# A two-block layer on one Trainium2 core: first unit in pieces of 1 to 4 rows behind zero products, later norm, earlier rotation tables, k as the third unit

## The reference

```python
u = rmsnorm(h, g_mix[i])
proj = u @ w_in[i]
q, k, v, z, xbc, dt_raw, g_a, g_s = jnp.split(proj, offsets, axis=-1)
q = apply_rope(q..., positions)
k = apply_rope(k..., positions)
attn = sliding_window_sink_attention(q, k, v, sinks[i])
```

## Time and profile before

| | us |
|---|---|
| median of 3 runs | 2734.81 |
| lowest, highest | 2734.21, 2738.23 |
| the profiled execution's own time | 2736.75 |
| its span | 2734.9 |
| PE busy | 2702.9 |
| DVE busy | 1961.5 |
| ACT busy | 1412.4 |

### The profile page before, as it was taken

One profiled execution on the slowest core, in us unless ns is written; L12 is line 12 of the kernel. 1 busy time (PEld: TensorE's weight loads), 2 busy tenths in 40 slices (PEclk: granted clock), 3 DMA queues, 4 the chain that ended last, 5 costly groups with the idle time before them and its releaser, 6 DMA issues.

```text
span 2734.9 us, 41656 instructions
## 1 busy us (share of the span) xinstructions
PE 2702.9 (99%) x16606; PEld 2375.4 (87%) x16606; DVE 1961.5 (72%) x2946; ACT 1412.4 (52%) x2092; POOL 105.5 (4%) x197
## 2 busy tenths in 40 slices
PE   8999999999999999999999999999999999999998
PEld 7888888888888888888888899998888888888887
DVE  7668777757777776677766778877787775677764
ACT  6455556544555554455544552257665553455543
POOL 1320000000000000000000000000000000000000
PEclk9999999999999999999999999999999999999999
DMA  7566556555578888877856556973455556555554
GB/s 241 168 206 208 179 177 207 187 189 188 185 238 281 286 279 299 293 279 277 278 201 213 176 184 223 314 264 116 139 185 190 192 194 191 186 188 185 187 194 143
DMA packets 168914, 581.58 MB, mean 213 GB/s; under 512 B 20128, under 2 KB 26992, under 8 KB 168208
## 3 DMA queue, kind: packets, MB, share of 16 engines
q1 hardware_dynamic: 152368, 526.06, 57.4%
q0 software_dynamic: 16208, 52.85, 5.2%
q10 hardware_dynamic: 144, 0.01, 0.0%
HBM read 535.06 MB, written 43.09 MB: 211 GB/s over the span
## 4 chain that ended last, share of the span: by engine, by line
PE 93%; DVE 3%; DMA 2%; ACT 1%; issue 1%; POOL 0%; SPq 0%; DVEq 0%; ACTq 0%; POOLq 0%
PE PS L957 92%; DVE wl L1922 1%; DMA raw<-in_w_in 1%; PE PS L1295 0%; DVE SQA L1922 0%; DVE H L1922 0%; DVE QT L1922 0%; ACT wh L1380 0%; DMA RO<-KT 0%; PE PS L1122 0%; DMA raw<-in_w_down 0%; ACT AHt L1380 0%; DMA KDU<-KT 0%; DVE CC L1930 0%; DMA H<-in_xT 0%
## 5 line engine op out<-in xcount | busy, mean ns | idle before, releaser
L1922 DVE TENSOR_TENSOR wl<-raw,wh 128x1024 fp32r<-128x1024 f32 (+3 forms) x888 | 1039.8, 1195 | 447.9 <-ACT wh L1380 446.1
L1380 ACT ACTIVATE wh<-raw 128x1024 fp32r<-128x1024 f32 (+3 forms) x888 | 894.3, 1031 | 521.7 <-PE PS L957 407.9
L957 PE MATMUL PS<-CHt,wh 128*128 128x512 f32 x2816 | 885.8, 395 | 0.0
L957 PE MATMUL PS<-BIGt,wh 128*128 128x512 f32 (+1 forms) x2816 | 756.0, 356 | 1.8 <-issue 0.6
L957 PE MATMUL PS<-AHt,wh 128*128 128x512 f32 (+1 forms) x2080 | 636.0, 386 | 11.4 <-DVE wl L1922 11.3
L957 PEld LDWEIGHTS PS<-CHt,wl 128*128 128x128 f32 x2816 | 529.0, 188 | 124.8
L957 PE MATMUL PS<-CHt,wl 128*128 128x256 f32 x2816 | 553.5, 278 | 0.0
L957 PEld LDWEIGHTS PS<-BIGt,wl 128*128 128x128 f32 x2304 | 435.4, 189 | 79.0 <-issue 0.2
L957 PE MATMUL PS<-BIGt,wl 128*128 128x256 f32 x2304 | 498.4, 279 | 0.0
L957 PEld LDWEIGHTS PS<-BIGt,wh 128*128 128x128 f32 x2816 | 434.9, 190 | 6.5 <-issue 3.8
L957 PEld LDWEIGHTS PS<-AHt,wl 128*128 128x128 f32 x1952 | 367.8, 188 | 79.8 <-issue 0.7
(11 more groups left out here) (311 smaller groups left out, 1632.0 us busy)
## 6 DMA issues: line engine op xcount, KB each, us to landing
raw<-in_w_up SPq DMA_DIRECT2D x264, 512.0 KB, 5.0
raw<-in_w_in SPq DMA_DIRECT2D x196, 512.0 KB, 4.1
raw<-in_w_down SPq DMA_DIRECT2D x132, 512.0 KB, 4.3
raw<-in_w_gate SPq DMA_DIRECT2D x88, 512.0 KB, 5.5
raw<-in_w_down SPq DMA_DIRECT2D x56, 384.0 KB, 3.5
PKR<-in_w_in SPq DMA_DIRECT2D x36, 512.0 KB, 5.2
parked_halves<-PKH POOLq DMA_DIRECT2D x36, 512.0 KB, 5.7
parked_halves<-PKL POOLq DMA_DIRECT2D x36, 512.0 KB, 7.0
```

What stands on the lines that cost most here:

```text
L957: return e.matmul(o, l, r, start=start, stop=stop, skip_group_check=True)
L1380: return e.activation(o, x, f, **k)
L1922: return e.tensor_tensor(o, x, y, op)
```

## The change

The first unit is cut into seven pieces of 1, 1, 2, 4, 4, 2 and 2 rows (`FIRST`) in place of four of 4, and the loads of x are cut the same way; the first two of x are issued by ScalarE, the others by SyncE between the weight loads. PE begins with three products of a tile of zeros (`WARM`), which GpSimd fills first. GpSimd's loads of constants wait for the last of x, where they waited for its second quarter. The norm and the first unit's finish stand five pieces after its end (`QHOLD`), the second unit's finish two. The rotation tables are put in the same lane as the sums of x, behind them. k is the third unit; the bank pairs keep their order, so that k gets (2,0). The turned copies of q and k get slots to match (`TURN_Q`), and some semaphores are merged.

```diff
+FIRST = (1, 1, 2, 4, 4, 2, 2)
+WARM = 3
-QHOLD = 3
+QHOLD = 5
...
-    for i in range(4):
-
-        add("w_in", 0, 16, 256 * i, "U1", "ev_q", i, mode=order(i), mid=(("norm", 0, 0),) if i == 0 else (), hold=QHOLD if i == 0 else 0,
-            banks=((0, 1), (3, 4), (2, 0), (1, 3))[i],
-            gens=([2, stage("rotary", 0, 3)] if i == 0 else []) + [("rope_q", i, [None] * (0 if i else 2) + [0, None, 1])])
-    add("w_in", 0, 16, 1024, "U1", "ev_k", 0, mode="turn", banks=(4, 2), gens2=[stage("full_u1", 0, 4)], gens=[("rope_k", 0, [0, None, 1, 2, None])])
+    first_banks = iter(((0, 1), (3, 4), (2, 0), (1, 3), (4, 2)))
+    for what in ("q0", "q1", "k", "q2", "q3"):
+        if what == "k":
+            add("w_in", 0, 16, 1024, "U1", "ev_k", 0, mode="turn", banks=next(first_banks), gens=[("rope_k", 0, [0, None, 1, 2])])
+            continue
+        i = int(what[1])
+        add("w_in", 0, 16, 256 * i, "U1", "ev_q", i, mode=order(i), mid=(("norm", 0, 0),) if i == 0 else (),
+            hold=(QHOLD, 2, 0, 0)[i], banks=next(first_banks), gens2=[stage("full_u1", 0, 4)] if i == 3 else [],
+            gens=[("rope_q", i, [0, None, 1])])
...
-    side.extend([stage("sum_x", 0, 4)])
+    side.extend([2, stage("sum_x", 0, 4, len(FIRST) - 2), stage("rotary", 0, 3, len(FIRST) + 1)])
...
     def pool_program(e):
+        e.memset(SQA[:, :, :], 0.0).then_inc(filled.sem)
...
-        e.wait_ge(x_in[1], 16)
+        e.wait_ge(x_in[-1], 16)
...
+            elif i == 2:
+                e.wait_ge(rq_d.sem, rq_d.at(1, "q"))
             else:
-                e.wait_ge(rot_a.sem, rot_a.at(0, "aex"))
+                e.wait_ge(rot_a.sem, rot_a.at(0, "cos"))
...
+        e.wait_ge(filled.sem, 1)
+        still = SQA[:, :, :].rearrange("p a b -> p (a b)")
+        for _ in range(WARM):
+            mm(PS[:, 7, :], SQA[:, 0, 0:P], still)
...
         e.dma_start(CV[:, 0:16], a["vecs"][:, 0:16]).then_inc(g_in, 16)
 
+        for i in range(2):
+            load_x(e, i)
```

More of the change, by code:

```diff
@@ L313, in pieces @@
             step = NSUB * 256 // (u.nc if len(ms) == 2 else P)
-            subs += [(n, ms, k, min(step, u.nk - k)) for k in range(0, u.nk, step)]
+            if n == 0:
+                subs += [(n, ms, sum(FIRST[:j]), c) for j, c in enumerate(FIRST)]
+            else:
+                subs += [(n, ms, k, min(step, u.nk - k)) for k in range(0, u.nk, step)]
     a = next(s for s, x in enumerate(subs) if us[x[0]].rhs == "U2")
@@ L339, in make_plan @@
     nf, ns = NRAW, 0
-    for s in range(4):
+    for s in range(len(FIRST)):
         plan.append(("seed", s, 0))
         plan.append(("split", s, 0))
-        ns += 1
+        plan.append(("fetch", nf, 0))
+        nf, ns = nf + 1, ns + 1
     full = {s for s, x in enumerate(subs) if us[x[0]].mode == "full"}
@@ L634, in hybrid_block_kernel @@
     raw_in = [dma(f"raw{i}") for i in range(NRAW)]
-    g_in, cv_in, mats_in, mask_in, row_in, pos_in = (dma(n) for n in ("g_mix", "cv", "mats", "mask", "row", "pos"))
-    x_in = [dma(f"x{i}") for i in range(4)]
+    g_in, cv_in, mats_in, row_in = (dma(n) for n in ("g_mix", "vecs_positions_then_x_again", "mats", "row_and_mask"))
+    x_in = [dma(f"x{i}") for i in range(len(FIRST))]
     dist_out, head_out, query_out, cbi_in, bm_in, p_in, w2_in = (
@@ L639, in hybrid_block_kernel @@
     xc_in = dma("blocks")
[L640 removed]
+    filled = steps("filled")
     w1_in = [dma("w1k"), dma("w1v")]
@@ L756, in hybrid_block_kernel, with load_x @@
     LN_READ = {0: "mean", 5: "rs", 8: "sp"}
+    def load_x(e, i):
+        k, c = sum(FIRST[:i]), FIRST[i]
+        src = a["xT"][P * k:P * (k + c), :].rearrange("(t p) n -> p t n", p=P)
+        e.dma_start(H[:, k:k + c, :], src).then_inc(x_in[i], 16)
     def sync_program(e):
[L760 to L764, removed]
         for kind, s, _ in plan:
@@ L802, in sync_program @@
             e.dma_start(RAW[s % NRAW][:, 0:w], src).then_inc(raw_in[s % NRAW], 16)
-            if s < 3:
-                load_x(s + 1)
+            if 1 <= s < len(FIRST) - 1:
+                load_x(e, s + 1)
         for i in range(8):
@@ L863, in rope_q @@
             e.wait_ge(evq_d.sem, evq_d.at(i))
-            if i >= 2:
-                e.wait_ge(rq_d.sem, rq_d.at(i - 2, "q"))
-            else:
-                e.wait_ge(rot_a.sem, rot_a.at(0, "aex"))
-            turn_heads(RQ[i % 2], QT[:, 2 * i:2 * i + 2, :], rq_in[i % 2])
+            if i == 3:
+                e.wait_ge(rk_d.sem, rk_d.at(0, "k"))
+            elif i == 2:
+                e.wait_ge(rq_d.sem, rq_d.at(1, "q"))
+            else:
+                e.wait_ge(rot_a.sem, rot_a.at(0, "cos"))
+            slot = TURN_Q[i][0]
+            turn_heads(RQ[slot], QT[:, 2 * i:2 * i + 2, :], rq_in[slot])
         def rope_k(t, ph):
@@ L1437, in seed @@
             e.wait_ge(x_in[i], 16)
-            for k in range(4 * i, 4 * i + 4):
+            for k in range(sum(FIRST[:i]), sum(FIRST[:i + 1])):
                 af(x.hi(k), H[:, k, :], ACT.Copy, scale=vec("g_mix", k)).then_inc(x.hi_made.sem)
@@ L1964, in gather @@
                     e.wait_ge(nrm_pe.sem, j)
+                else:
+                    e.wait_ge(sub_done.sem, 1)
                 if j == 5:
@@ L2031, in rope_q @@
         def rope_q(i, ph):
-            o, x = QT[:, 2 * i:2 * i + 2, :], RQ[i % 2]
+            slot, turn = TURN_Q[i]
+            o, x = QT[:, 2 * i:2 * i + 2, :], RQ[slot]
             if ph:
-                e.wait_ge(rq_in[i % 2], 64 * (i // 2 + 1))
+                e.wait_ge(rq_in[slot], 64 * turn)
                 tt(x, x, two(SIN[:, :]), MUL).then_inc(rq_d.sem)
@@ L2285, in ev_h @@
             if i == 0:
-                e.wait_ge(x_again, 32)
+                e.wait_ge(x_again, 64)
             if i >= 8 and i < 24:
```

29 lines of the change are left out of this document (13 added, 16 removed).

## The result

The change makes the kernel slower by 0.34%, which is clear of the noise: 2743.85 us in the median (2741.85 to 2747.41, 6 runs) against 2734.45 (2733.31 to 2738.23, 6 runs) for the kernel before beside it. The ratio is 1.0034, with a 95% interval of 1.0024 to 1.0044. Forecast were 2739.7 and at most 2742.5, so the sign was right, the size was too small by about half (4.9 us for 9.4), and the measured median lies above the forecast's range. The profiled execution took 2745.39 us at a span of 2743.6, 8.7 more than before.

A forecast was written before the change was run, and what follows sets the result against it. PE, busy 2702.9 of 2734.9 us, was taken as the bound. A 6.6 us later passage, less 3.1 of stalls, plus 1.4 of clock gave +4.9 on the median 2734.81: 2739.7 us, range 2734.6 to 2742.5.

The forecast's parts named there:

- The place and the mechanism of the wait: At the third unit's second half PE waits for bank 0 until VectorE's join at 47.3 us: 8.8 us.
- The first unit: PE starts at about 6.3 us, the fourth piece at 12.5, and the unit ends at 20.8 instead of 22.7.
- The start of VectorE's chain: VectorE starts piece 9's `wl` at 22.8 us (21.6 to 25.3), with 4.9 us for its weight transfer.
- a longer wait: Rival: GpSimd's constants delay the weights of pieces 8 and 9, the chain starts at 24.7: +6.8 us, 2741.6; chance 0.18 with late pieces.
- From there to the join: VectorE's sums 5.8, tables 4.4 and six `wl` 6.8 us, then `COS` to the join, ending at 47.3 us.
- The tail: From `COS` at 39.8 us: 2.9 us and a `wl` of 1.14, then factor, root, reciprocal and join, 3.4 us.
- The clock: After the 8.8 us wait PE restarts at half clock and loses 1.4 us (0 to 1.7).
- The stalls that go: PE's stalls at 59.15 (1.4 us) and 91.66 (1.7 us) vanish with tables ahead and k third: 3.1 us.
- ScalarE's table load: Between `COS` and the exponential, priced without a drain; a drain of 1.4 us would make the sum +6.3.
- The upper end of the range: Whole kernel +7.7 us, or 2742.5, the top of the range holding 8 of 10.

The follow-up runs named there:

- the second run of the changed kernel: The changed kernel run again with nothing altered, to see how far its stretches repeat: median 2743.83 us, ratio 1.0035.

## Why the forecast had the sign and missed the size

- *The place and the mechanism of the wait* were right: one wait, for `QT`, at the third unit's second half, none for `KDU`, none near 59. Tables behind the join (landmark 100.27 to 92.15) shows it.
- *The first unit*: first piece at 5.58 (forecast 6.3), the fourth at 12.48 (12.5). PE was ready for the waiting product at 40.1 (38.5; the last product's record ends at 40.27): the norm waited 1.16 us for the sums, which I had not priced. It didn't count, since the join was later.
- *The start of VectorE's chain* is the step that failed. I took 22.8 for piece 9's `wl`, with 4.9 us for the transfer; the issue was right (16.7, forecast 16.8), but the transfer took 7.0 and `wl` started at 24.79. Piece 10's took 8.8 and brought another 0.90, for which the sum had no term. I had written the cause down as the rival "a longer wait", with a start at 24.7, and gave it 0.18, arguing that fewer bytes are queued then. That argument failed: holding the constants back gave 47.28. My upper bound, 6.7 us, was also read from the wrong row. It is of a transfer issued at 15.9, 3 us behind the last constant (12.3 to 12.9). Piece 9's is issued in the midst of the constants, and the nearest row of before is that of the transfer issued at 13.1, 8.2 us (shown below the list). This step is worth 2.0 + 0.9 = 2.9 us.
- *From there to the join*: forecast 47.3 - 22.8 = 24.5 us. Measured 50.3 - 24.8 = 25.5, of which 0.9 is piece 10. The tail (`COS` to the join, 7.5 us) came out as 50.3 - 42.8 = 7.5.
- *The clock* was mis-sized: 1.4 forecast with 1.7 as the bound, from the start of before. Filling the wait measured 2.3 (1.9 against the second run of the changed kernel). The runs with a wait of 6.5 to 10 us there lost 1.3 to 2.3 by the same reckoning (48.99 to 49.95 from join to landmark, against 47.67). The rule of the Trainium skill (TensorE: Matmul & The Clock Gate, Part 1), an idle PE falls to half clock, agrees with the trace: PEclk 0.51 and 0.50 in the two windows.
- *The stalls that go*: 3.1 us forecast; with it the sum closes within 0.1. That PE passed the point at 40.7 before was right too (40.8). The run with k fifth shows that a wait for `KDU` costs clock beside its length, if it is 3.40 us long.
- *ScalarE's table load* took from 43.22 to 44.52, and the exponential followed at once. The Trainium skill (ScalarE: Activation LUTs, What ACT_TABLE_LOAD costs) adds a drain of about 1.4 us; as in the earlier trace rows the trace has none, and the measurement decides.

The transfer of before that was issued at 13.1:

```profile
raw<-in_w_in SPq DMA_DIRECT2D x1, 512.0 KB, 8.2
```

With the two sizes put right the forecast's own sum gives 4.9 + 2.9 + 0.9 = 8.7, the measured difference of the spans. The upper end of the range, +7.7, took a join at 49.8 and 1.7 us of clock; measured were 50.3 and 2.3 to 2.4.

As to what the parts are worth once nothing else is in the way: k third gains 2.2 us at the landmark and 4.9 with the slow products behind it, small pieces 3.4 to 4.5 against large ones in the new order of loads, but only 0.4 to 1.5 against the start of before. The zeros gained nothing in either pair of runs, and the tables' new place costs 8 us. The wait swallowed the gain of the start and outweighed that of k.

## What to carry to other kernels

Before pulling work forward, follow the engine that has to deliver the next shared thing (here VectorE, with the join that frees a bank); an earlier start of the consumer is worth nothing while that chain is late. Here what was put ahead of it, the tables with ScalarE's part, cost its whole length (the join 7.4 us later), and a load of constants is such a thing too: beside it the transfer that started the chain took 7.0 us and not 4.4, so place it where the chain no longer waits for transfers. When a transfer's time is taken from an old trace, take the row with the same neighbours in the queue. Count a long idle time of TensorE as longer than it is (here 1.3 to 2.3 us for 6.5 to 10). And compare each part with the kernel that it replaces: small pieces looked worth 4.5 us against a start that the change itself had made 3 us later.

## What the runs showed of the hardware

- The clock fell after shorter idle times than I had thought. In the first 100 us of these runs it stayed at 1.00 after 1.0 to 1.6 us wherever such a wait stood alone. Of nine idle times between 2.0 and 2.5 us six were followed by a fall (2.23: 0.84 and 0.82 in the windows of 5 us around and behind it; 2.48: 0.86 and 0.79), three were not (2.06 with k fifth, 2.21 in the changed kernel, 2.05 at 82.01 with other banks). At 3.40 and more, with work ahead of the wait, it fell each time, to 0.50.
- Half pace lasted 2.9 to 4.9 us behind a wait of 6.5 to 10 us, with no relation to its length in these runs: 4.9 and 3.6 us in two runs of the same kernel.
- Where PE has done nothing yet, the granted clock reads 1.00 although the products run at half pace (0.77 at 5.86 us). What tells it there is the pace alone.
- A transfer of 512 KB took 7.0 to 9.0 us beside about 1 MB of constants, where those just before and behind took 3.5 to 4.6. When the constants were issued 9.6 us later, the slow transfers came later too (7.4 us for one issued between 26 and 27).
